# Delta rule: where the sums of squared queries and keys, the levels and the last third of the last outputs stand in the order of work

## The reference, cut to what matters

```
q = l2_norm(q) * 128 ** -0.5        # x * rsqrt(sum(x*x) + 1e-6), per head and token
k = l2_norm(k)
beta = sigmoid(beta_pre);  g = -exp(a_log) * softplus(a_pre + dt_bias)
o = chunk_gated_delta_rule(q, k, v, g, beta)    # per chunk: (I + A) x = rhs, then a scan over chunks
o = rms_norm(o, w_norm) * silu(z)
h = h + o @ w_out                   # the outputs' product
...
h = h + squared_relu_mlp(rms_norm(h, ffn_norm), ff_up, ff_down)
```

## Time and profile before

| | |
|---|---|
| profiled execution, its own time | 4029.49 us |
| its span, first to last instruction | 4027.7 us |
| TensorE (PE) busy | 3715.6 us, 92% |
| VectorE (DVE) busy | 2607.9 us, 65% |
| ScalarE (ACT) busy | 1525.8 us, 38% |
| GpSimd (POOL) busy | 802.1 us, 20% |
| mean granted TensorE clock | 0.962 |
| delta rule, steps 0 to 9 | 1973.7 to about 2880 us |
| its last outputs | 2881.7 to about 2908 us |
| the matrix memory's last outputs | 3615.9 to about 3642 us |

### The profile page before, as it was taken

One profiled execution on the slowest core, in us unless ns is written; L12 is line 12 of the kernel. 1 busy time (PEld: TensorE's weight loads), 2 busy tenths in 40 slices (PEclk: granted clock), 3 DMA queues, 4 the chain that ended last, 5 costly groups with the idle time before them and its releaser, 6 DMA issues. The chain is left out here.

```text
span 4027.7 us, 60638 instructions
## 1 busy us (share of the span) xinstructions
PE 3715.6 (92%) x24575; PEld 3443.4 (85%) x24575; DVE 2607.9 (65%) x5091; ACT 1525.8 (38%) x2724; POOL 802.1 (20%) x661
## 2 busy tenths in 40 slices
PE   7999989889989999999889998888899999979999
PEld 5777869889989999999688888887799999979999
DVE  4664337999977999999567666766542434465342
ACT  4555223345543333333443333332441424444241
POOL 0000004557752333333022121221000001110000
PEclk9999999999999999999889999999899999989999
DMA  3112223458888899999142322331122311112221
GB/s 116 63 63 74 93 74 122 142 167 274 276 268 310 316 328 337 327 330 332 58 66 55 60 49 58 60 60 28 64 85 83 100 48 60 62 46 86 91 92 59
DMA packets 208150, 542.33 MB, mean 135 GB/s; under 512 B 18664, under 2 KB 92904, under 8 KB 207872
## 3 DMA queue, kind: packets, MB, share of 16 engines
q1 hardware_dynamic: 99792, 341.22, 24.9%
q0 software_dynamic: 42048, 150.49, 13.5%
q10 hardware_dynamic: 66032, 46.75, 3.7%
HBM read 492.14 MB, written 46.25 MB: 134 GB/s over the span
## 5 line engine op out<-in xcount | busy, mean ns | idle before, releaser
L96 PE MATMUL bank<-Xh,wh 128*128 128x272 f32 (+3 forms) x3680 | 1228.9, 334 | 33.9 <-DVE Xl L123 16.4
L96 PE MATMUL bank<-Xl,wh 128*128 128x272 f32 (+3 forms) x3680 | 1161.0, 315 | 0.0
L96 PE MATMUL bank<-Xh,wl 128*128 128x272 f32 (+3 forms) x3680 | 1160.0, 315 | 0.0
L123 DVE TENSOR_TENSOR wl<-raw,wh 128x1024 fp32r<-128x1024 f32 (+1 forms) x536 | 581.9, 1104 | 457.0 <-ACT wh L117 453.1
L117 ACT ACTIVATE wh<-raw 128x1024 fp32r<-128x1024 f32 (+1 forms) x632 | 588.7, 953 | 657.2 <-PE bank L96 605.5
L96 PEld LDWEIGHTS bank<-Xh,wh 128*128 128x128 f32 x3680 | 708.7, 193 | 101.3 <-issue 56.3
L96 PEld LDWEIGHTS bank<-Xl,wh 128*128 128x128 f32 x3680 | 709.4, 193 | 18.9 <-issue 2.0
L96 PEld LDWEIGHTS bank<-Xh,wl 128*128 128x128 f32 x3680 | 706.4, 192 | 20.6
L123 DVE TENSOR_TENSOR H<-H,bank 128x384 f32<-128x384 f32 (+3 forms) x522 | 251.3, 491 | 322.6 <-PE bank L96 321.0
L96 PE MATMUL bank<-aah,wh 128*128 128x384 f32 x1024 | 355.7, 347 | 41.8 <-DVE aal L123 16.5
L123 POOL TENSOR_TENSOR wl<-raw,wh 128x1024 fp32r<-128x1024 f32 x96 | 281.4, 2934 | 521.8 <-ACT wh L117 521.3
(11 more groups left out here) (314 smaller groups left out, 6170.3 us busy)
## 6 DMA issues: line engine op xcount, KB each, us to landing
raw<-in_u SPq DMA_DIRECT2D x128, 512.0 KB
raw<-in_v SPq DMA_DIRECT2D x128, 512.0 KB
raw<-in_up SPq DMA_DIRECT2D x64, 512.0 KB, 3.6
raw<-in_down SPq DMA_DIRECT2D x64, 512.0 KB, 3.4
scratch<-gb ACTq DMA_DIRECT2D x12, 2048.0 KB, 13.9
gj<-scratch SPq DMA_DIRECT2D x32, 768.0 KB, 7.8
raw<-in_w_gdn SPq DMA_DIRECT2D x48, 512.0 KB
raw<-in_w_att SPq DMA_DIRECT2D x36, 512.0 KB
```

The lines of the kernel that those rows point to most:

```text
L96: return Issued(self, self.q and self.q.matmul(out, l, r, start=start, stop=stop), 1)
L123: return Issued(self, self.q and self.q.tensor_tensor(out, a, b, op), 1)
```

## The change

Three edits. (a) The sums of squared queries and keys go from 12 to 16 dense steps behind their slab, the inverse roots from 14 to 17, the scaling from 16 to 19. (b) For every pair but the first, `levels_gdn` begins with an empty step, and its length is given as 38. (c) The last third of the last outputs becomes a generator, `last_third` and `last_third1`, which `last_outputs` advances once behind each group: in the delta rule sums, inverse root and product with z behind the first group, gate and split behind the third; in the matrix memory behind the second and the fourth. `last_outputs` prepares weights behind groups 5, 6, 7 and 8 of the first half, no longer behind 2, 4, 6 and 8.

```diff
--- before.py
+++ after.py
@@ -1158,7 +1158,7 @@
 
         FFH, FFL, FTR, LAST_DOWN, ROOM = {}, {}, {}, {}, {}
 
-        def last_outputs(layer, names, xs, signal, ring):
+        def last_outputs(layer, names, xs, signal, ring, chain):
 
 
             ws = [slab(*n) for n in names]
@@ -1175,6 +1175,7 @@
                     do("resid", g, fb, a, b)
                     given_back(g, "resid", g)
                     behind.append((a, fb, "resid", g))
+                    next(chain, None)
                     if len(behind) > 2:
                         sums_part(key, *behind.pop(0))
                     if hf and fb == 1:
@@ -1183,7 +1184,7 @@
                         for k in ((fb - 3) * 2, (fb - 3) * 2 + 1):
                             if k < 8:
                                 norm_block(key, *HALVES[0], k, ring=ring)
-                    if not hf and fb % 2 or hf and fb == 0:
+                    if not hf and fb > 3 or hf and fb == 0:
                         prepare(1)
             for x in behind:
                 sums_part(key, *x)
@@ -1366,9 +1367,9 @@
                                 after(4 - tap, lambda p=p, n=n, tap=tap: convolve(p, n, tap))
                             if n < 2:
                                 after(8, lambda p=p, n=n: l2_squares(p, n))
-                                after(12, lambda p=p, n=n: [sums_now(("l2", p, n, hf)) for hf in range(2)])
-                                after(14, lambda p=p, n=n: [do("rms_inv", ("l2", p, n, hf)) for hf in range(2)])
-                                after(16, lambda p=p, n=n: l2_scale(p, n))
+                                after(16, lambda p=p, n=n: [sums_now(("l2", p, n, hf)) for hf in range(2)])
+                                after(17, lambda p=p, n=n: [do("rms_inv", ("l2", p, n, hf)) for hf in range(2)])
+                                after(19, lambda p=p, n=n: l2_scale(p, n))
                             else:
                                 after(8, lambda p=p, n=n: silu_v(p, n))
                         step()
@@ -1400,6 +1401,8 @@
 
         def levels_gdn(p):
             TB.take(p), KE.take(p)
+            if p:
+                yield 1
             do("keys_twice", p)
             for g in range(2):
                 do("decay", p, g)
@@ -1534,19 +1537,25 @@
             if t == 0:
                 streams.append((gates_gdn(), 22))
             if 0 <= t - 1 < 8:
-                streams.append((levels_gdn(t - 1), 37))
+                streams.append((levels_gdn(t - 1), 37 + (t > 1)))
             if t > 1:
                 streams.append((scans(t), 8 * (t > 2) + 26 * (t < 10)))
             merge(*streams)
-        sums_now(("out", 7, 2))
-        do("rms_inv", ("out", 7, 2))
-        do("times_z", ("out", 7, 2))
-        do("gdn_gate", 7, 2)
-        for e in range(2):
-            do("gdn_split", 7, e, 1)
+
+        def last_third():
+            sums_now(("out", 7, 2))
+            do("rms_inv", ("out", 7, 2))
+            do("times_z", ("out", 7, 2))
+            yield
+            yield
+            do("gdn_gate", 7, 2)
+            for e in range(2):
+                do("gdn_split", 7, e, 1)
+            yield
+
         room_at = gdn_end - 7 * 1152
         ROOM[0] = room_at, more_room(("up0", "down0"), 1, 3, (("so", 7, 8), ("vnm", 7, 8), ("sn", 7, 7, 1)), room_at)
-        last_outputs(0, [("gdn_out", 14), ("gdn_out", 15)], OX.at[7], "ogl", XQ7)
+        last_outputs(0, [("gdn_out", 14), ("gdn_out", 15)], OX.at[7], "ogl", XQ7, last_third())
         ffn(0)
 
 
@@ -1782,15 +1791,22 @@
             merge(*streams)
         divided(3, 2)
         ml_squares(3, 2)
-        sums_now(("mout", 3, 2))
-        do("rms_inv", ("mout", 3, 2))
-        do("times_z", ("mout", 3, 2))
-        do("ml_gate", 3, 2)
-        for e in range(2):
-            do("ml_split", 3, e, 1)
+
+        def last_third1():
+            yield
+            sums_now(("mout", 3, 2))
+            do("rms_inv", ("mout", 3, 2))
+            do("times_z", ("mout", 3, 2))
+            yield
+            yield
+            do("ml_gate", 3, 2)
+            for e in range(2):
+                do("ml_split", 3, e, 1)
+            yield
+
         room_at = base + 19072
         ROOM[1] = room_at, more_room(("up1", "down1"), 1, 3, (("mo", 3, 8), ("msn", 3, 7), ("mnum", 3, 2)), room_at)
-        last_outputs(1, [("ml_out", 6), ("ml_out", 7)], OX1.at[3], "mogl", XQ3)
+        last_outputs(1, [("ml_out", 6), ("ml_out", 7)], OX1.at[3], "mogl", XQ3, last_third1())
         ffn(1)
         do("store")
```

## The result

The changed kernel took 4085.13 us (median of 4 runs, 4079.22 to 4090.68) beside 4028.7 for the kernel before on the same chip (4 runs, 4025.72 to 4030.6): ratio 1.0141, 95% interval 1.0123 to 1.0158. It is 56 us slower, where 20 us faster was forecast, and it lies outside the range. The profiled execution has a span of 4088.9 us against 4027.7. The delta rule's full steps are the larger part of it: steps 3 to 7 took 106.4 to 107.9 us each before and 114.9 to 116.2 after, 42.9 together. Steps 1 and 2 lost another 18.5. Step 0 gained 2.7, steps 8 and 9 came out even. That is 58.6 of the 61.2 us between the two spans.

The account below looks back on a forecast made before the run. TensorE, 92% busy, was taken to bound the kernel through its work, waits and half clock. Terms 2.5 + 1.0 + 13 - 0.5 + 1.4 + 2.2 = 19.6 us gave 4007.5 us, range 3991 to 4025.

Parts of the forecast that it names:

- The failed step: Late part of a full delta-rule step: no TensorE wait over 0.3, so the net gain of 2.6 us a step stays.
- the new wait: TensorE after the sums of squares, for a PSUM bank freed by ScalarE's Ln: 0.85 us a step.
- The sums: Sums of squares in a full step: taps end at 2441.5 or 2443.2, wait for rt 1.2 in place of 4.92.
- The gain at the product of vd and tb: Mid-step in the delta rule: TensorE gets there 4.4 or 2.7 us earlier than before.
- a sign of being wrong: Listed marks against the forecast: rt waits over 3 us, a ta wait over 4, or step starts costing under 3.
- The start: Start of full steps: GpSimd's keys' copy ends at 2422.3, so a wait of 3.19 becomes about 5, a loss there.
- Step 0: Delta rule's first step: more products ahead of the sums shorten a 6.19 us wait; 2.5 us gained, 0 to 4.
- Steps 1 and 2: Early delta-rule steps: the first gains 0, the second 1.0 us (0 to 2) on its 5.19 wait for the values.
- The tails: Last outputs: delta rule gains 1.4 us (-1 to 3), matrix memory 2.2 (0 to 4).
- The slower one: Full steps: keys' copy behind `times_z` delays pairs and taps; a step loses 3, 8.4 us slower, 4035.5; chance 0.10.
- Given back at ta: Full steps: TensorE next waits for the first ta, steps keep their time, only 6.6 us remain: 4020.5; chance 0.22.
- The port: VectorE and GpSimd exclude each other at `decay` 2: a step's gain is the lower 1.8, 4 us less in all.

Follow-up runs that it names:

- e2: Kernel before with only the level step one step later for every pair but the first: 4034.86 us, ratio 1.0032.
- e12: Kernel before with the level step one step later, but GpSimd's copy of the keys issued ahead of that extra step: 4008.65 us, ratio 0.9963.
- e3: Kernel before with only the changed tails, the last third beside the product and weight splits in groups 5 to 8: 4026.83 us, ratio 1.0005.
- e13: Kernel before with later level step, keys' copy left ahead of it, and sums, roots, scaling at 14, 14, 16: 4014.29 us, ratio 0.997.
- e14: Kernel before with later level step, keys' copy left ahead of it, and sums, roots, scaling at 15, 15, 17: 4008.42 us, ratio 0.9962.
- e4_roots_at_18: Changed kernel, all three edits, with the inverse roots at 18 in place of 17: 4057.31 us, ratio 1.0085 to the kernel before.
- e7_all_s16_18_21: Changed kernel with sums, roots and scaling at 16, 18, 21: 4052.14 us, ratio 1.0062 to the kernel before.
- e6: Changed kernel with sums, roots and scaling at 14, 15, 17: 4037.83 us, ratio 1.0027 to the kernel before.

## Why the prediction was wrong

- **The failed step** is "From 2449 on TensorE had no wait over 0.3, so the gain is kept". That was true of the old order. The moved roots were issued into that very stretch, and I looked there only for TensorE's own waits. The prediction even has the queue in hand, in the new wait ("the Ln, now behind the copy of the key slab's end: copy 0.4, load 1.28, Ln 0.5"), but follows from the roots only to who waits for the roots. What stood behind them on ScalarE, wh, and behind that on VectorE, was never asked. From the product of vd and tb to the end of the step it measured 10.3 us in place of the 0.85 of the one new wait.
- **The new wait** of 0.85 was 0.86.
- **The sums** came with no wait for rt (predicted 1.2), the taps' end at 2476.15, in the old step's time 2442.5 (2441.5 or 2443.2), right. The gain at the product of vd and tb was 2.3 (4.4 or 2.7). What lacks there is the wait for ta: 4.37, over the 2 to 3.7 given (a wait over 4 was named as a sign of being wrong), and with half clock in and behind it (2473.3 to 2480.0), which I had put at none.
- **The start** came as worked out: a wait of 4.71 at the keys for one of about 5, the copy 2454.45 + 1.13, in the old time 2421.9 for 2422.3. I had called it a loss; e2 gives 13 us for it in all, e12 shows that it was wholly the copy's place.
- **Step 0** gained 2.7 (2.5). **Steps 1 and 2**, put at 0 and 1.0, lost 18.5: each of their slabs whose roots moved has the wait for wh too (2.15, 3.03, 3.02 and 3.02 in the changed kernel), and TensorE's 5.19 for the values in step 2 became 5.65 for vn.
- **The tails** were put at 3.6 and gave nothing (e3: 1.0005). From the outputs' sums at 2864.99 to the sums of squares at 2901.71 the delta tail took 36.72 us before and 36.67 in e3; from the sums at 3600.59 to those at 3641.83 the matrix memory's took 41.24 and 42.46. The wait for ro went in the delta tail and shrank from 8.18 to 2.83 in the other, and new ones came: 1.73 for wl, 2.68 for sq, in e3's delta tail

```profile
2874.26 0.39 PE L96 MATMUL bank<-ogh,wh 128*128 128x272 f32 x1 [1.73 <-DVE wl L123]
...
2879.71 1.28 PE L96 MATMUL bank<-sq,ones 128*128 128x272 f32 x2 [2.68 <-ACT sq L117]
```

  with 3.4 us of half clock behind the second (2879.4 to 2882.8). The old wait for ro had covered the one for wl; the squares stand behind the split that waits for the gate, here too ("Tails" above).
- **The rivals.** The slower one, by GpSimd's place, exists and is worth 13 us, but not by the way it names: in the changed kernel the taps did not end at 2445. "Given back at ta" is what e13 and e14 show once nothing else is in the way. The range ended below the result since no rival priced ScalarE's queue.
- **The port.** The prediction's lower bound took the three dd of `decay` 2 at 2.57. They took 2.35 in the changed kernel and 3.23 in e12, with GpSimd at work beside them, where six took 1.66 at a place without it. What it did not price is the other side: the level step moves GpSimd's product away from the four wl, 4.48 to 2.50. In the changed kernel that gives nothing, since the pairs then wait for the keys; in e12 it counts. The rule of "SBUF — State Buffer", section "SBUF: two separate sides", in the Trainium skill agrees with all of these; the level step moves other work as well, so no run shows the port alone.

## What to carry to other kernels

When an operation is moved later, write out its engine's queue at the new place, and ask for every instruction that then stands behind it who waits for that, one engine further too. Most of all around the points where the next buffer is prepared. A move that frees one wait is worth only what the next one in line leaves; moving the cause (here one copy on another engine) was worth more than moving the waiting instruction. And an order of work can carry two moves of which one alone is the gain: try them apart.

## What the runs showed of the hardware

- A wait of 1.9 to 2.7 us on TensorE had 3.4 to 6.8 us at clock 0.50 behind it (3.4 behind 2.50 and 2.66 in the changed kernel and behind 1.90 in e4_roots_at_18, 6.8 behind 1.89 in e7_all_s16_18_21), so such a wait cost up to nearly three times its length. The same wait of 4.71 for the keys had 3.4 in and behind it in e6 and 6.8 in e7. Yet the 2.67 in the kernel before had none in the 1.6 us until the next wait; what tells them apart is open.
- Four wl of VectorE took 4.48 us beside a GpSimd product in the kernel before, and 2.84 (e12) and 2.50 (changed kernel) with GpSimd's product elsewhere.
- The table load took 1.28 us, and the next operation started 0.02 us after its end (2482.14 and 2483.44). The Trainium skill, "ScalarE: Activation LUTs", section "What ACT_TABLE_LOAD costs", adds 1.38 us for a drain to each switch; the trace shows none here, neither behind the load nor ahead of it (the copy before it ends at 2482.13, the load starts at 2482.14).
